# Moving an attention operand off the residual stream, and contracting its matmuls over 64 and 65 rows instead of 128

## The reference

```python
def dilated_group_attention(q, k_cat, v_cat, dil, w_phase):
    s = jnp.einsum("bpnihd,bpnjhd->bpnhij", qb, k_cat)      # contraction over d, 64 features
    s = jnp.where(valid, s, -jnp.inf)
    lse = jax.nn.logsumexp(s, axis=-1)
    p = jnp.exp(s - lse[..., None])
    o = jnp.einsum("bpnhij,bpnjhd->bpnihd", p, v_cat)

x = x + dilated_attention(rms_norm(x, b_norm), w_q, w_o, kv)   # x is the residual stream
```

## Time and profile before

| | us |
|---|---|
| median of 3 runs | 1849.31 |
| lowest and highest | 1847.35 and 1853.51 |
| the profiled execution's own time | 1853.51 |
| span of its trace | 1851.7 |
| the loop over head pairs in it, from its first matmul to its last | 753.7 to 1389.4 |
| PE busy in the span | 1562.5 (84%) |

### The profile page before, as it was taken

The page is one execution under the profiler, slowest core; times in us unless marked ns, Lnnn a source line. Parts: engine busy times, 40 slices in busy tenths (PEclk is TensorE's granted clock), DMA queues, the critical chain, the costliest instruction groups (busy, mean ns, idle before and its releaser), DMA issues. The chain is left out here.

```text
span 1851.7 us, 19289 instructions
## 1 busy us (share of the span) xinstructions
PE 1562.5 (84%) x6688; PEld 1171.9 (63%) x6688; DVE 1170.6 (63%) x1426; ACT 702.0 (38%) x762; POOL 509.6 (28%) x430
## 2 busy tenths in 40 slices
PE   6868048499999993799999999999998569999992
PEld 3323027367776662688888888888887556667760
DVE  2999992565666653848576574766643575656653
ACT  3323441245546551442232323323232335555541
POOL 2677700222222322314042240413310022322220
PEclk8988569589999996899999999999999679999996
DMA  3430000248887874212021211212111647888854
GB/s 151 188 136 21 25 0 30 114 162 356 356 364 324 341 310 186 93 58 70 32 81 55 68 57 45 79 45 69 55 57 70 288 150 294 343 371 350 368 228 158
DMA packets 44846, 303.08 MB, mean 164 GB/s; under 512 B 9488, under 2 KB 10256, under 8 KB 30992
## 3 DMA queue, kind: packets, MB, share of 16 engines
q1 hardware_dynamic: 34304, 284.98, 39.0%
q0 software_dynamic: 9648, 16.80, 2.5%
q10 hardware_dynamic: 864, 0.94, 0.1%
HBM read 295.34 MB, written 25.69 MB: 173 GB/s over the span
## 5 line engine op out<-in xcount | busy, mean ns | idle before, releaser
L626 POOL TENSOR_TENSOR KQ<-rope_ab 64x512 f32<-64x512 f32 x96 | 172.6, 1798 | 431.7 <-DVE rope_ab L1223 428.1
L1132 DVE TENSOR_TENSOR wgl<-WR,wgh 128x2048 fp32r<-128x2048 f32 x66 | 148.2, 2288 | 175.7 <-ACT wgh L741 172.8
L1404 PE MATMUL PS<-WR,SC 128*128 128x512 f32 x528 | 233.2, 594 | 4.1 <-ACT SC L775 3.2
L807 ACT ACTIVATE wh<-wraw 128x1024 fp32r<-128x1024 f32 x80 | 84.4, 1058 | 276.2 <-PE PS L1460 253.1
L1404 PEld LDWEIGHTS PS<-WR,SC 128*128 128x128 f32 x528 | 98.8, 190 | 118.3 <-issue 116.4
L1306 PE MATMUL PS<-HT,WR 128*128 128x512 f32 x256 | 123.5, 647 | 36.0 <-DVE SC L917 34.0
L928 DVE SCALAR_TENSOR_TENSOR SC<-SC 128x512 f32<-128x512 f32 x144 | 153.2, 1134 | 0.0
L1132 DVE TENSOR_TENSOR wul<-WR,wuh 128x2048 fp32r<-128x2048 f32 x66 | 148.0, 2283 | 0.3 <-ACT wuh L741 0.3
L741 ACT ACTIVATE wgh<-WR 128x2048 fp32r<-128x2048 f32 x66 | 122.4, 1904 | 62.0 <-DMA WR<-w_gate 62.0
L741 ACT ACTIVATE wuh<-WR 128x2048 fp32r<-128x2048 f32 x66 | 122.7, 1906 | 31.1 <-PE PS L1378 20.7
L1223 DVE TENSOR_TENSOR rope_ab<-PS,rope_sb 32x512 f32<-32x512 f32 x192 | 131.9, 687 | 2.6
(11 more groups left out here) (245 smaller groups left out, 3322.4 us busy)
## 6 DMA issues: line engine op xcount, KB each, us to landing
WR<-w_gate SPq DMA_DIRECT2D x33, 2048.0 KB, 12.3
WR<-w_up SPq DMA_DIRECT2D x33, 2048.0 KB, 16.8
WR<-w_down SPq DMA_DIRECT2D x33, 2048.0 KB, 14.0
wraw<-w_qkv SPq DMA_DIRECT2D x72, 512.0 KB, 3.3
WR<-w_in SPq DMA_DIRECT2D x8, 1024.0 KB, 4.8
WO<-w_out SPq DMA_DIRECT2D x1, 4096.0 KB, 14.8
xn_dram<-HTQ SPq DMA_DIRECT2D x8, 512.0 KB, 2.6
HT<-y_dram SPq DMA_DIRECT2D x8, 512.0 KB, 6.5
```

Source lines behind the costliest of these rows:

```text
L626: ins = nc.gpsimd.tensor_tensor(dst[h][0:HEAD, g, :], rope_ab[rows, 2 * (t % 2), :], rope_ab[rows, 2 * (t % 2) + 1, :], ALU.add)
L1132: V.tensor_tensor(lo[:, kts, :], raw[:, kts, :], hi[:, kts, :].bitcast(F32), ALU.subtract).then_inc(done, 1)
L1404: ins = M.matmul(PS[3 + h][:, :], hidT[:, ft, :], wd[b][:, ft, h * 512:(h + 1) * 512], start=ft == 0, stop=ft == FT - 1)
```

## The change

`QKh` moves from offset 0 to offset 176 KiB, over `Pm`. So `X` stays in place through the attention, and its store to `x_dram`, its read back, the DRAM buffer and the waits for both are gone. The products of `scores` contract over rows 0 to 63 alone, those of `scores_t` over rows 0 to 64, and the two fills with zeros are gone. A semaphore's name is replaced by another that nothing uses.

```diff
-    x_dram = nc.dram_tensor("x_dram", (T, D), F32).ap()
...
-        QKh = at("QKh", 0, [P, 2, NG, T], F32R)
+        QKh = at("QKh", 176, [P, 2, NG, T], F32R)
...  # SP
-            for n in range(NT):
-                sp.wait_ge(x_upd.sem, x_upd.at("kv", n + 1))
-                sp.dma_start(x_dram[n * P:(n + 1) * P, :], X[:, n, :]).then_inc(x_spilled, 16)
...
-            sp.wait_ge(s1_mm, 8 * NP_HEADS)
-            for n in range(NT):
-                sp.dma_start(X[:, n, :], x_dram[n * P:(n + 1) * P, :]).then_inc(x_in[n], 16)
...  # POOL
-            steps.step(nc.gpsimd.memset(KQ[HEAD:P, :, :, :], 0.0))
             for h in range(2):
                 steps.step(nc.gpsimd.memset(Kh[h][HEAD:HEAD + 1, :, :], 1.0))
-            pool.wait_ge(x_spilled, NT * 16)
-            pool.wait_ge(xn_ready.sem, xn_ready.at("kv", NT))
-            steps.step(nc.gpsimd.memset(QKh[HEAD:P, :, :, :].bitcast(F32), 0.0))
...  # DVE
-            for n in range(NT):
-                dve.wait_ge(x_in[n], 32)
...  # PE, scores
-  ins = M.matmul(PS[4 + s][:, at:at + w], q[:, g, tile_of(g, n)], k[:, g, keys],
+  ins = M.matmul(PS[4 + s][:, at:at + w], q[0:HEAD, g, tile_of(g, n)], k[0:HEAD, g, keys],
...  # PE, scores_t
-  ins = M.matmul(PS[4 + s][:, at:at + w], k[:, g, tile_of(g, n)], q[:, g, queries],
+  ins = M.matmul(PS[4 + s][:, at:at + w], k[0:HEAD + 1, g, tile_of(g, n)], q[0:HEAD + 1, g, queries],
```

More of the change, by code:

```diff
@@ L389, in build_program @@
         pairs_done, row_done = sem("pairs_done"), sem("row_done")
-        rope_ab_done, hi_done, oTh_done, oTl_done, x_spilled = (sem(s) for s in ("rope_ab_done", "hi_done", "oTh_done", "oTl_done", "x_spilled"))
+        rope_ab_done, hi_done, oTh_done, oTl_done, o_free = (sem(s) for s in ("rope_ab_done", "hi_done", "oTh_done", "oTl_done", "o_free"))
         rope_done, v_done = (sem(s) for s in ("rope_done", "v_done"))
```

## The result

The changed kernel takes 1915.13 us by its median (1896.52 to 1921.34, 4 runs) against 1850.26 for the kernel before (4 runs): 1.035 times as long, 95% interval 1.0291 to 1.0409. It is 65 us slower, where 0.7 us less was forecast. Its executions also spread over 25 us, those of before over 6.

A forecast was written before the change was run, and what follows sets the result against it. PE was taken to bound the loop, DVE's chain the border before it. The terms, -0.7 us for the earlier start and 0 for all others, gave 1848.6 us against the median of 1849.3; range 1842 to 1860.

The forecast's parts named there:

- The border before the loop: DVE's chain before PE's first projection: without the `KQ` fill the second norm scale ends 0.94 us earlier, taken as -0.7 us.
- The first scale: DVE's first norm scale before the loop, waiting out POOL's `Vs` fill: claimed to stay near 2.8 us.
- rival D: Before the loop: the removed store was in the way, read-backs land 1.3 us earlier, 1847.3 us; chance 0.04.
- the read of `X`: Border behind the loop: removing the read gains 0, since the output product covers it with 16.6 us to spare.
- The new place of `QKh`: In the loop, sharing bytes with `Pm`: no wait added and none later, by order, so 0.
- the contraction over 64 and 65 rows: PE's `scores` and `scores_t` products in the loop: taken at 0, between -16 us and +22 us.
- The far end: Upper bound for fewer rows in `scores`: 128 changes of rows, each losing 0.17 us of overlap, +22 us.
- rival A: Each change of contracted rows in `scores` empties PE: at 0.17 us a change 1870 us, at a third 1856; chance 0.24.
- the step from the one-column products to the masks: Nearest shape change, at the row of maxima: step 0.11 us, under a mask product's 0.221, so the array is not emptied.
- rival C: The granted clock falls to half during `scores`, with half the rows at rest: +48 us, 1896 us; chance 0.02.
- Rival B: Fewer rows are faster on PE in the loop: up to -16 us, 1832 us, with a third of it 1843; chance 0.12.

The follow-up runs named there:

- the run with the small products: Kernel before plus one 64-row product by a single zero column in each bank of `scores`, all other products over 128 rows: 1894.73 us, ratio 1.0231.

## Why the prediction was wrong

**The border before the loop: right.** The start of PE was forecast 0.94 us earlier, and 0.92 was measured. The part of it that reaches the end was taken as 0.7; no run is fine enough to show that. The first scale stayed at 2.83, no delay of the read-backs by the store stands out from their scatter (rival D), and the read of `X` was hidden.

**The new place of `QKh`: right.** The waits of PE are the same 11.0 us, and with full rows the time is that of before. The three signs of being wrong that the prediction named (a longer step from mask to product, a trip over 79.5 us, a clock below 1.00) all came.

**The step that failed is the last part, the contraction over 64 and 65 rows, taken at 0.** It has three errors.

First, the price of a change from 128 to 64 rows. The far end was 0.17 us and 22 us in all; the runs show 0.155 to 0.16 us on average and 20.5 us, nearly rival A's price. I took 0 because the step from the one-column products to the masks showed no pause. That row was a change of columns, and it says nothing of rows. The Trainium skill's rule in "TensorEngine Tiling (Array Packing)", Key Properties, that a change of mode drains TensorE, was cited for rival A. The trace agrees with it for 64 rows, by 0.155 to 0.16 us a change. 65 rows bring no such pause.

Second, the clock, rival C, had a chance of 0.02, since "the clock is 1.00 through the trip, one-column products and waits included". That trip had full rows and no changes of rows, so it could not speak against the rival. Nor does it hold for all trips: in trip seven of the kernel before the clock does fall, in the first head's scores, which start at 1269.77 behind PE's wait.

```profile
1271.00:1276.00 5.00, 5.00 (x21) 4.48 (x21) 3.80 (x7) 2.83 (x4) 0.00 (x0) 0.66 0.32 105
```

I also looked for the fall during `scores` only. It comes there or behind them, and lasts 3 to 7 us for each head; most of what it costs is in the value projections, which the change does not touch. A trip is 6.35 us longer, of which the changes of rows are 16 x 0.16 = 2.6 and the low clock the other 3.8.

Third, I counted none for `scores_t`, since 65 rows need more than half the array. For pauses that holds; for the clock it does not. Over 65 rows it costs 23 us in the kernel before and 46 in the changed kernel with its `scores` at 65 rows.

The rivals were also taken one at a time. The clock falls with A's changes of rows, as the run with the small products shows, so A and C were one case. Their prices alone were 22 and 48 us, and that the measured 65 is near to both together is luck: the 48 stood for half clock in all of `scores` and nowhere else. The runs put 46 to 48 us on `scores` over 64 rows, changes and low clock together, and up to 24 more on the executions in which the clock falls at `scores_t` too. Rival B (faster) is out: the products start 0.23 us apart over 64 rows as over 128, and their weight loads last 0.28 us on average in both runs with masks first.

**What stays open.** How much of `scores_t` and what follows runs at half clock depends on something else than its 65 rows: the same products gave 7 us a trip in one kernel and 17 in another, and none in most trips of three of the four profiles of the changed kernel. Where in the trip the fall comes repeats from trip to trip within an execution and differs between executions. I did not find what sets it, nor why 96 rows are enough. Five quite different kernels have the same trip within 0.05 us, 85.26 to 85.31 us: four with eight changes of rows a head, and the one with 65 rows in both, which has no change to 64 rows at all. So equal times do not show equal causes here, and what a part costs alone need not be what it costs beside the others. The 9 us of low clock in the run with 64 rows and masks first may come from its two pauses a head or from its 64-row products; no run parts them.

## What to carry to other kernels

Fewer contracted rows save PE nothing, and can cost twice: by a pause of 0.16 us at each change between 64 and 128 rows, and by the clock of what follows. Where rows are free, fill them with zeros and keep one shape, which cost nothing here. Grouping the products by shape, so that the changes are few, took the loss from 48 us to 14. And when a change touches the densest stretch of the bounding engine, price the clock behind it as well as the instructions in it.

## What the runs showed that I had not expected

- The granted clock fell from 2.4 to 1.2 GHz while PE was busy without a gap, some 4 us (in one kernel) or 10 us (in another) into fp32 products over 65 rows. Over 96 or 128 rows, the same products kept it at 2.4 GHz.
- Eight changes of rows within 4.4 us, each with a pause of some 0.1 us, were followed by half clock for some 3 us, with all wide products over 128 rows.
- The kernel before loses its full clock too, in one trip of eight, in the scores behind PE's wait of 1.38 us. In the two kernels with all 128 rows that lay all masks of a head first, behind that wait or before it, no trip shows it.
- One one-column product before the products of each bank cost 0.14 us (0.56 us for four), though its own step is 0.02 to 0.03 us: the step from a 512-wide mask to what follows it grew from 0.04 and 0.06 to 0.23 and 0.25 us.
